# High and low weights interleaved word by word in SBUF, and all weights 128 bytes further from their moving rows

## What is computed

```python
def _swiglu(x, wg, wu, wd):
    return (jax.nn.silu(x @ wg) * (x @ wu)) @ wd

for l in range(DEPTH):
    h = x + 0.5 * _swiglu(_rmsnorm(x, ffn1_norm[l]), ffn1_wg[l], ffn1_wu[l], ffn1_wd[l])
    u = _rmsnorm(h, mix_norm[l])
    p = u @ w_in[l]
    rq, rk, rv, rg, dq, dk, dv = jnp.split(p, splits, axis=-1)
    ret = _retention(rq, rk, rv, rg, ret_decay_logit[l], ret_gn_g[l])
    dif = _diff_attn(dq, dk, dv, ...)
    h = h + jnp.concatenate([ret, dif], axis=-1) @ w_out[l]
    h = h + 0.5 * _swiglu(_rmsnorm(h, ffn2_norm[l]), ffn2_wg[l], ffn2_wu[l], ffn2_wd[l])
    x = _rmsnorm(h, final_norm[l])
```

## Time and profile before

| | |
|---|---|
| time of the kernel, median of 2 runs | 1838.16 us (1837.28 to 1839.04) |
| time of the profiled execution | 1838.71 us |
| its span, first to last instruction | 1836.9 us |
| PE busy | 1820.7 us (99%), 12,744 matmul records |
| PEld busy | 1691.2 us (92%) |
| DVE, ACT, POOL busy | 1374.3 (75%), 1017.6 (55%), 1349.2 us (73%) |
| granted TensorE clock, mean | 0.999 |
| DMA | 186.73 MB, 29.3% of the 16 engines' time on the SP queue |

### The profile page before, as it was taken

The page is one execution under the profiler, slowest core; times in us unless marked ns, Lnnn a source line. Parts: engine busy times, 40 slices in busy tenths (PEclk is TensorE's granted clock), DMA queues, the critical chain, the costliest instruction groups (busy, mean ns, idle before and its releaser), DMA issues. The chain is left out here.

```text
span 1836.9 us, 33605 instructions
## 1 busy us (share of the span) xinstructions
PE 1820.7 (99%) x12744; PEld 1691.2 (92%) x12744; DVE 1374.3 (75%) x2409; ACT 1017.6 (55%) x1770; POOL 1349.2 (73%) x880
## 2 busy tenths in 40 slices
PE   9999999999999999999999999999999999999998
PEld 7999999887888999999889999998778889999997
DVE  7888886656755887888688888767477468888874
ACT  7656555456425655555575465555564266555553
POOL 6998897465445898988479998955544368999883
PEclk9999999999999999999999999999999999999999
DMA  4433333222223233323234233323222132333332
GB/s 152 152 112 119 115 123 103 89 95 69 69 69 115 77 109 115 109 99 110 79 112 139 96 113 116 100 85 115 80 69 70 58 115 97 111 116 105 103 113 72
DMA packets 56461, 186.73 MB, mean 102 GB/s; under 512 B 6600, under 2 KB 10440, under 8 KB 56300
## 3 DMA queue, kind: packets, MB, share of 16 engines
q1 hardware_dynamic: 54000, 181.09, 29.3%
q10 hardware_dynamic: 2300, 3.48, 0.6%
HBM read 182.44 MB, written 3.15 MB: 101 GB/s over the span
## 5 line engine op out<-in xcount | busy, mean ns | idle before, releaser
L679 POOL TENSOR_TENSOR w<-raw,w 128x512 fp32r<-128x512 f32 (+1 forms) x194 | 259.6, 1361 | 215.6 <-ACT w L1289 215.5
L1369 ACT ACTIVATE bank<-bank 128x512 f32<-128x512 f32 x88 | 51.1, 581 | 236.7 <-DVE bank L1951 236.7
L788 PE MATMUL bank<-hg_hi,w 128*128 128x512 f32 x436 | 174.1, 399 | 0.0
L790 PE MATMUL bank<-hg_hi,w 128*128 128x512 f32 x436 | 170.1, 390 | 0.0
L789 PE MATMUL bank<-hg_lo,w 128*128 128x512 f32 x436 | 170.1, 390 | 0.0
L1289 ACT ACTIVATE w<-raw 128x1024 fp32r<-128x1024 f32 (+1 forms) x97 | 98.8, 1023 | 118.9 <-PE bank L790 95.7
L706 POOL TENSOR_TENSOR w<-raw_x,w 128x1024 fp32r<-128x1024 f32 x56 | 135.1, 2413 | 26.3 <-ACT w L1314 26.3
L951 PE MATMUL bank<-hg_hi,w 128*128 128x256 f32 x960 | 151.6, 280 | 0.0
L953 PE MATMUL bank<-hg_lo,w 128*128 128x256 f32 x960 | 151.5, 280 | 0.0
L956 PE MATMUL bank<-hg_hi,w 128*128 128x256 f32 x960 | 151.3, 279 | 0.0
L688 POOL TENSOR_TENSOR w<-raw_x,w 128x1024 fp32r<-128x1024 f32 x56 | 136.0, 2429 | 16.2 <-ACT w L1306 16.1
(11 more groups left out here) (363 smaller groups left out, 5697.1 us busy)
## 6 DMA issues: line engine op xcount, KB each, us to landing
raw<-in_w_gu SPq DMA_DIRECT2D x96, 512.0 KB, 3.9
raw_x<-in_w_gu SPq DMA_DIRECT2D x80, 512.0 KB, 4.4
raw<-in_w_p SPq DMA_DIRECT2D x56, 512.0 KB, 3.2
raw_x<-in_w_dn SPq DMA_DIRECT2D x32, 512.0 KB, 4.4
raw<-in_w_dn SPq DMA_DIRECT2D x32, 512.0 KB, 4.2
raw<-in_w_o SPq DMA_DIRECT2D x16, 512.0 KB, 3.3
raw_x<-in_w_dn SPq DMA_DIRECT2D x16, 384.0 KB, 3.9
raw<-in_w_dn SPq DMA_DIRECT2D x16, 384.0 KB, 3.5
```

What stands on the lines that cost most here:

```text
L679: ins = pool.tensor_tensor(columns(lo_[:, part, :]), source[:, part.start * P:part.stop * P], columns(hi[:, part, :]).bitcast(F32), ALU.su ...
L788: pe.matmul(out, hi[:, 0, :], m_hi, start=first, stop=False)
L790: return pe.matmul(out, lo_[:, 0, :], m_hi, start=False, stop=last)
```

## The change

The high and the low part of a unit no longer lie in two areas. They are interleaved: word 2i of a unit's 8,192 bytes is the high part of weight i, word 2i + 1 its low part. `w_tiles` returns two views of the same stretch with a step of two words. So every weight load reads 128 words at a step of 8 bytes, over 1,024 bytes instead of 512; ACT, POOL and DVE write, and POOL and DVE read, the parts with the same step.

Two tensors of 32 words (128 bytes) are added that nothing uses: phase ahead of w, phase_x behind w_x. w now starts 74,080 bytes behind hg_hi (96 modulo 256). w_x starts 16,544 bytes ahead of mix_hi, which stays where it was (again 96 modulo 256). Weights used through `block_tiles` stand 96 from their moving rows modulo 256, those used through `w_tiles` 128. The tensors between w and w_x, and those that share their space with w_x in the attention part, start 128 bytes earlier than before.

```diff
-W_AT = (0, UT * P, 2 * UT * P, 3 * UT * P + SPACER)
-W_PART = SLOTS * UT * P + SPACER
-X_PART = 2 * UT * P
+UNIT = 2 * UT * P
+W_AT = (0, UNIT, 2 * UNIT, 3 * UNIT + SPACER)
 GAP = 56
+PHASE = 32
...
-        w = sb("w", [P, 2 * W_PART + PLAIN_AT], F32R)
+        sb("phase", [P, PHASE])
+        w = sb("w", [P, SLOTS * UNIT + SPACER + PLAIN_AT], F32R)
...
-            w_x = sb_ffn("w_x", [P, 2 * X_PART + PLAIN_AT], F32R)
+            w_x = sb_ffn("w_x", [P, 2 * UNIT + PLAIN_AT], F32R)
+            sb_ffn("phase_x", [P, PHASE])
...
         def w_tiles(s, n=UT, at_=0, shift=PLAIN_AT):
 
-            buffer, part, first = (w, W_PART, W_AT[s]) if s < SLOTS else (w_x, X_PART, (s - SLOTS) * UT * P)
-            first += shift + at_ * P
-            hi, lo = buffer[:, first:first + n * P], buffer[:, part + first:part + first + n * P]
-            return hi.rearrange("p (a b) -> p a b", b=P), lo.rearrange("p (a b) -> p a b", b=P)
+            buffer, first = (w, W_AT[s]) if s < SLOTS else (w_x, (s - SLOTS) * UNIT)
+            first += shift + 2 * at_ * P
+            both = buffer[:, first:first + 2 * n * P].rearrange("p (a b two) -> p a b two", b=P, two=2)
+            return both[:, :, :, 0], both[:, :, :, 1]
```

## The result

The changed kernel takes 1882.8 us (median of 2 runs, 1881.29 to 1884.3) against 1838.16: a ratio of 1.0236, with a 95% interval of 1.022 to 1.0253. It is slower by 45 us. Its profiled execution took 1881.29 us.

A forecast was written before the change was run, and what follows sets the result against it. The prediction took PE to bound the kernel, by matmul count times spacing. Its terms, each taken as 0, summed to 0 on the profiled 1838.71 us, giving 1838 us, with a range from 1795 to 2025 us.

The forecast's parts named there:

- What bounds the kernel: Whole kernel: PE is busy 1820.7 of 1836.9 us, so time is the number of matmuls times their spacing.
- The load as the floor of 117 ns: 256-wide matmuls: a weight load's own 0.11 us plus a few ns sets their 117 ns, not the moving rows.
- (a): Weight loads reading every second word: taken as 0 ns; upper bound, the load's 0.11 us doubles.
- (b): Interference of weight load and moving-row reads: taken as 0; best 34 us won, worst +151 and +34 us.
- Rival 1: Matmuls: the doubled load read collides with the moving row, full price 2023 us; chance 0.20 between small and full price.
- The 107 ns for 256 columns, and the 13 ns left at both widths: Matmul spacing: 256 columns cost 107 ns, 512 cost 214; the 13 ns left are the most interference can cost.
- Rival 4: Matmuls: the fixed distance between the two reads ends all interference, 1795 us, 2.3% faster; chance 0.09.
- (c): All weights 128 bytes further from their moving rows: taken as 0; 28 us if every 256-wide matmul went to 0.120 us.
- (d): Copies and subtractions on ACT, DVE and POOL at every second word: taken as 0, POOL's slack 0.98 us a block.
- Rival 2: Blocks: POOL's strided instructions become the bound, 1954 us, or 2179 us if both double; chance 0.12.
- Rival 3: Weight loads: the load itself slows to half, 231 ns for a 256-wide matmul, 2911 us; chance 0.13.
- The two rules weighed: Strided reads: two hits per 16-byte line suffice (1838), against full rate only for adjacent pairs (87 ns on a load).

The follow-up runs named there:

- c_phase32: The kernel before, high and low parts still in two areas, with all weights 128 bytes further from their moving rows: 1863.2 us, ratio 1.013.
- b_pairs: The kernel before with only the blocks' weight loads reading every second word (8-byte step, products mix tiles): 1866.93 us, ratio 1.0157.
- r_pairs: The kernel before with neighbouring tiles interleaved by the host, so only weight loads have a step of two words, copies stay contiguous: 1880.9 us, ratio 1.0225.
- i_phase0: The changed kernel without its 128 bytes, so interleaved at the distances of before: 1884.53 us, ratio 1.0242.
- w_spread: The kernel before with only ACT, POOL and DVE accessing the parts at a step of two words, weight loads contiguous: 1844.22 us, ratio 1.0028.
- r_quads: As r_pairs, but four tiles interleaved, so nearly all weight loads have a step of 16 bytes: 2945.5 us, ratio 1.6015.

## Why the prediction was wrong

The time lies in the range, but the likeliest case, no measurable change, did not come. Step by step:

- **What bounds the kernel**: right. PE's spacing times the number of matmuls accounts for the result, and no other engine came near it. A PE that keeps its 99% while the 256-wide spacing moves by 4 ns or more was named as the way to fall. It moved by 3.6 ns, just short of that; the threshold spread the whole 37 us over the 256-wide matmuls and left out the 512-wide ones, which moved by 4.2.
- **The load as the floor of 117 ns**: borne out in the main. With 12 and 16 bytes of step the spacing follows the load. But the load is not alone at 117 ns: c_phase32 moves the blocks to 118.45 ns and the lone load stays at 187.
- **(a) Strided loads, 0 ns**: this is the step that failed, a cost put at nothing. The argument was that passing 1,024 bytes in 0.11 us is what the moving read does anyway. It took the load to be able to do what the moving read does, and no row showed that. The load is slower at it: +7 ns on a lone load, +9 in the crowd, +3.3 ns on the spacing, 29 us in blocks alone (b_pairs); at 12 and 16 bytes it passes 16 bytes in 1.8 ns, by which 1,024 bytes take 115. The term's upper bound, a doubled load, is what a step of 16 bytes does.
- How 7 to 9 ns on a load become 3 on the spacing stays open. In the stream, the next matmul starts on average 114 ns behind the load's start before and 116 after, so it doesn't wait for all of the load's recorded 188 or 197 ns. But where nothing moves beside it, the matmul gets longer by more than its load: the first one of the first block, which follows a lone load, lasts 356 ns before and 367 after, 11 more (one line of the kernel before, then one of the changed one, duration ns min/median/max):

```profile
L951 PE MATMUL bank<-mix_hi,w x1: 356/356/356, 38.8 to 38.8; 128*128 128x256 f32 x1
L953 PE MATMUL bank<-mix_hi,w x1: 367/367/367, 39.5 to 39.5; 128*128 128x256 f32 x1
```

- **(b) Interference, 0**: in blocks nothing beyond the load's own cost is seen. At 512 columns it was mis-sized: 4.2 ns, 11 us, where the sum had 0 and the worst case 13 ns, 34 us. The reason given, that it stays below the loads' floor, holds for 256-wide matmuls alone; the 512-wide ones have no such floor, and r_pairs costs them 5.9 ns at the same distance. Rival 1 had the right kind of loss there at a third of its price.
- **The 107 ns for 256 columns, and the 13 ns left at both widths**: never shown. 107 is the difference between a spacing that the load sets and one that it doesn't, and it changes with the distance: 227.3 - 119.9 = 107 ns at 0, 229.1 - 117.8 = 111 at 192, 233.3 - 118.3 = 115 at 32. What a moving row of 256 takes by itself, and so how much interference there is to win, stays open; the fourth rival's price rests on it.
- **(c) 128 bytes further, 0**: right for the changed kernel (i_phase0 1884.5, after 1882.8), wrong as a statement on distance. With contiguous loads the same 128 bytes cost 24 us, near the bound of 28 worked out from the last stretch's 3 ns, but half of it at 512 columns, which that bound left out. The 3 ns themselves were read rightly: off distance 0 the last stretch gets faster by 1.3 to 2.1 ns and its loads by 3 to 4. Only the 512-wide ones go the other way.
- **(d) Copies, 0**: right but for 3 to 5 us of small pauses (w_spread; i_phase0 against r_pairs). ACT's 9 to 10% and POOL's 2% stay under cover for the rest; DVE shows none. POOL needed 0.38 ns more an element to become the bound and got 50 / 1,024 = 0.05. Rival 2 is refuted at a step of 8 bytes.
- **Rival 3, the load slows to half**: wrong for this change, but r_quads shows it with 16 bytes: 232.5 ns and 2946 us, where the rival had 231 ns and 2911.
- **Rival 4, the end of interference**: refuted at distances 0, 64 and 128 for the interleaved form (233.2, 230.4 and 231.5 ns, where it had 214). No distance that was run removes it.
- **The two rules weighed**: the first, of the Trainium skill's page "SBUF — State Buffer", was close to right and was taken too literally; a limit that is just met can still cost a few ns. The other, a hop at every element (the Trainium skill, "Vector Engine (DVE) Microarchitecture Reference", section 5.2), isn't seen at this step: DVE's L1896 takes 683 ns with a step of 8 bytes, 682 without, and the estimate by it of 87 ns on a load is ten times what came.
- **The chances**: slower had 0.45, but from rivals priced at 116 to 1,073 us. That the time still lies in the range, 1795 to 2025, is the width of the range and no merit of the sum. A loss of 3 to 4 ns a matmul had no case of its own, though the prediction itself wrote that 4 ns already decide. With 12,000 matmuls at the bound, "a few ns" deserved to be the likeliest case rather than exactly 0.

## What to carry to other kernels

Where float32r matmuls of 256 columns follow each other, each with a load of its own, the load is nearly the whole pace, and its access pattern is on the critical path. Keep stationary tiles contiguous. A step of 8 bytes cost such matmuls 3% here, 12 bytes 47%, 16 bytes 99%, so count the stretch that a load passes over and not the words that it uses. Longer matmuls do not hide this altogether: the 512-wide ones lost 2 to 3%. When a bound is thousands of equal instructions, cost a change of their access pattern by a few ns each before calling it nothing.

## What the runs showed of the hardware

- TensorE weight loads of 128 four-byte words in each partition: 187 ns alone when contiguous, 193 to 194 at a step of 8 bytes, 307 at 16; in the stream 188, 197, 261 (step 12) and 330 ns, with 117, 120, 172.5 and 232.5 ns between 256-wide matmuls. The last two are 1.8 ns for each 16 bytes passed.
- Where stationary tile and moving row lie relative to each other, modulo 256 bytes, moves 512-wide matmuls with contiguous loads by up to 6 ns (227.3 at 0, 229.1 at 192, 232.7 at 128, 233.3 at 32), though the record of a load (187 to 188 ns) ends before the next matmul starts. 256-wide ones of the last stretch move the other way: 119.9 at 0, 118.3 at 32, 118.6 at 128, 117.8 at 192. What in the two reads collides isn't known.
- A write with a step of 8 bytes costs ACT 9 to 10% (1,051 to 1,158 ns for 1,024 words), POOL's subtraction that also reads with it 2%, DVE's nothing.
